# Half of the modulation sums of an experts' stage, split between GpSimd and ScalarE

## The reference, cut to what matters

```python
# first block: 4 groups of 8 experts, d = 1024, d_expert = 256, 256 tokens
hdn = jax.nn.silu(jnp.einsum('td,edf->tef', xc, w1)) * jnp.einsum('td,edf->tef', xc, w3)
ffn = jnp.einsum('tef,efd->td', hdn * gate[:, :, None], w2)
x = layernorm(DEEPNORM_ALPHA * x + g2 * ffn, ln2_g[l], ln2_b[l])

# second block: one row vector times a 1024 x 9216 matrix in each layer
c_act = jax.nn.silu(c)
mod = (c_act @ ada_w[i] + ada_b[i]).reshape(bsz, N_SUB, 3, d)
```

## Time and profile before

| | |
|---|---|
| median of 3 runs | 3307.97 us |
| lowest and highest | 3305.1 and 3314.28 us |
| profiled execution, its own time | 3315.41 us |
| its span in the trace | 3313.6 us |
| mean granted TensorE clock | 0.935 of full speed |
| the 40 steps of the stage, by the trace | about 225 to 620 us of the span |

### The profile page before, as it was taken

How to read it: one execution, slowest core, us unless ns; L and a number is a source line. 1 busy time by engine, 2 the same in 40 slices (tenths; PEclk the granted TensorE clock), 3 DMA queues, 4 the chain that set the end, 5 groups by cost and what they waited for, 6 DMA issues and landing times. The chain is left out here.

```text
span 3313.6 us, 58520 instructions
## 1 busy us (share of the span) xinstructions
PE 3078.3 (93%) x23850; PEld 2755.8 (83%) x23850; DVE 2410.0 (73%) x3506; ACT 1701.3 (51%) x2514; POOL 137.8 (4%) x164
## 2 busy tenths in 40 slices
PE   8879999799988899999988999999999999988899
PEld 7667777699877789899977898998689898878798
DVE  7769999788675478787665587885678787674655
ACT  5447777554552355545555445544654555432444
POOL 0110000000102000000010000000000001011000
PEclk9779999899999799999987999999899999998899
DMA  9629999668310378585420586773068586300542
GB/s 359 267 98 389 361 367 370 251 265 309 122 64 4 119 273 307 226 309 226 180 115 10 200 309 256 279 292 144 39 265 313 218 310 235 117 2 7 192 187 81
DMA packets 80297, 699.00 MB, mean 211 GB/s; under 512 B 8875, under 2 KB 12971, under 8 KB 58956
## 3 DMA queue, kind: packets, MB, share of 16 engines
q1 hardware_dynamic: 33708, 525.98, 40.6%
q10 hardware_dynamic: 42912, 157.31, 12.6%
q0 software_dynamic: 3456, 12.58, 1.0%
HBM read 691.64 MB, written 4.19 MB: 210 GB/s over the span
## 5 line engine op out<-in xcount | busy, mean ns | idle before, releaser
L1060 ACT ACTIVATE w_split<-ring 128x1024 fp32r<-128x1024 f32 x513 | 541.1, 1058 | 659.0 <-PE banks L984 391.2
L1167 DVE TENSOR_TENSOR w_split<-ring,w_split 128x1024 fp32r<-128x1024 f32 x513 | 625.6, 1223 | 274.7 <-ACT w_split L1060 266.7
L980 PE MATMUL banks<-u_split,w_split 128*128 128x512 f32 x2816 | 751.0, 399 | 23.7 <-DVE u_split L1236 21.0
L980 PEld LDWEIGHTS banks<-u_split,w_split 128*128 128x128 f32 x2816 | 517.4, 192 | 127.1 <-issue 17.6
L984 PE MATMUL banks<-u_split,w_split 128*128 128x256 f32 x2816 | 436.5, 285 | 0.0
L984 PEld LDWEIGHTS banks<-u_split,w_split 128*128 128x128 f32 x2816 | 406.9, 194 | 25.0
L973 PE MATMUL banks<-h_split,w_split 128*128 128x256 f32 x1408 | 398.5, 283 | 0.0
L974 PE MATMUL banks<-h_split,w_split 128*128 128x256 f32 x1408 | 398.5, 283 | 0.0
L975 PE MATMUL banks<-h_split,w_split 128*128 128x256 f32 x1408 | 398.4, 283 | 0.0
L526 PE MATMUL banks<-bufs_split,ring_split 128*128 128x256 f32 x1376 | 397.7, 289 | 0.0
L590 DVE CUSTOM_DVE_ANT_0 bufs<-bufs 128x1024 f32<-128x1024 f32 x288 | 341.9, 1220 | 12.0 <-DVE w_split L1167 12.0
(11 more groups left out here) (516 smaller groups left out, 4961.8 us busy)
## 6 DMA issues: line engine op xcount, KB each, us to landing
ring<-stream SPq DMA_DIRECT2D x153, 3072.0 KB, 10.9
bufs<-ada ACTq DMA_DIRECT2D x296, 512.0 KB, 10.3
bufs<-ada POOLq DMA_DIRECT2D x19, 512.0 KB, 7.5
bufs<-ada SPq DMA_DIRECT2D x16, 512.0 KB, 8.6
ring<-stream SPq DMA_DIRECT2D x8, 768.0 KB, 10.2
ring<-stream SPq DMA_DIRECT2D x2, 2688.0 KB, 9.9
bufs<-c_rows SPq DMA_DIRECT2D x10, 512.0 KB, 4.4
ring<-stream SPq DMA_DIRECT2D x1, 2704.0 KB, 10.0
```

Of the source, the lines that this page charges most:

```text
L980: pe.matmul(bank, w_split[:, slot, 0, k * P:(k + 1) * P], u_split[:, k, :, :], start=(k == 0), stop=False, skip_group_check=True)
L1060: nc.scalar.activation(w_split[:, slot, 0, :], piece(j, b), ACT.Copy).then_inc(high.sem, 1)
L1167: e = nc.vector.tensor_tensor(w_split[:, slot, 1, :], piece(j, b), w_split[:, slot, 0, :].bitcast(F32), ALU.subtract)
```

## The change

Quarters with an even number stay as they are on VectorE. A quarter with an odd number is done in two instructions on two engines: GpSimd multiplies it by the row `c` in place, as soon as it has landed (`tensor_tensor`, 128 x 1024, both inputs in SBUF), and ScalarE copies it over itself with an accumulated output (`activation` with `accum_out`). ScalarE does this at the end of step `q + 1`, ahead of that step's load. GpSimd's eight additions keep their order among the products: a product stands ahead of an addition of the same step. The load of a quarter now waits for the sum of the one four before it on the engine that makes it. The addition of the bias for `g2` moves from the end of step 8 to the end of step 9.

```diff
+    def quarter_sum(q):
+        at = 5 * KC + q if q < gate_quarters else q - gate_quarters
+        return core.mod_sums[:, at:at + 1]
...
+        multiplied, odd_step = core.event("k_products"), core.event("gate_sums")
...
             def load_quarters(step_of):
                 for q in ada_quarters(step_of):
                     if q >= 4:
-                        act.wait_ge(step.sem, step.at(q - 3))
+                        summed = odd_step if q % 2 else step
+                        act.wait_ge(summed.sem, summed.at(q // 2 - 1))
...
+            def sum_odd_quarter(q):
+                act.wait_ge(multiplied.sem, multiplied.at(q // 2 + 1))
+                slot = ada_slot[:, (q % 4) * D:(q % 4 + 1) * D]
+                act.activation(slot, slot, ACT.Copy, accum_out=quarter_sum(q)).then_inc(odd_step.sem, odd_step.count(1))
...
                 if e == 5 and v < WINDOWS - 1:
                     window_high(v + 1)
+                for q in ada_quarters(j):
+                    if q % 2:
+                        sum_odd_quarter(q)
                 if j >= first_quarter:
                     load_quarters(j + 3)
...
-            for i in range(2 * WINDOWS - 2):
+            def add_scaled(i):
                 pool.wait_ge(y_scaled.sem, y_scaled.at(i + 1))
                 rows = core.x[:, 4 * (i % 2):4 * (i % 2) + 4, :].rearrange("p c t -> p (c t)")
                 pool.tensor_tensor(rows, rows, scaled_y, ALU.add).then_inc(x_added.sem, x_added.count(1))
+
+            pool.wait_ge(c_ready.sem, c_ready.at(1))
+            for j in range(1, units + 1):
+                v, e = divmod(j, E)
+                for q in ada_quarters(j):
+                    if q % 2:
+                        pool.wait_ge(ada_loaded[q % 4].sem, ada_loaded[q % 4].at(16 * (q // 4 + 1)))
+                        slot = ada_slot[:, (q % 4) * D:(q % 4 + 1) * D]
+                        pool.tensor_tensor(slot, slot, gate_c_row if q < gate_quarters else c_row, ALU.mult)\
+                            .then_inc(multiplied.sem, multiplied.count(1))
+                if e in (2, 3) and 1 <= v < WINDOWS:
+                    add_scaled(2 * (v - 1) + e - 2)
...
             def sum_quarter(q):
-                dve.wait_ge(ada_loaded[q % 4].sem, ada_loaded[q % 4].at(16 * (q // 4 + 1)))
-                if q < gate_quarters:
-                    ada_quarter(core, dve, q % 4, ada_slot, gate_c_row, core.mod_sums[:, 5 * KC + q:5 * KC + q + 1])
-                else:
-                    at = q - gate_quarters
-                    ada_quarter(core, dve, q % 4, ada_slot, c_row, core.mod_sums[:, at:at + 1])
-                if q == gate_quarters - 1:
-                    dve.wait_ge(step.sem, step.at(gate_quarters))
+                if q % 2 == 0:
+                    dve.wait_ge(ada_loaded[q % 4].sem, ada_loaded[q % 4].at(16 * (q // 4 + 1)))
+                    ada_quarter(core, dve, q % 4, ada_slot, gate_c_row if q < gate_quarters else c_row, quarter_sum(q))
+                if q == gate_quarters:
+                    dve.wait_ge(step.sem, step.at(gate_quarters // 2))
+                    dve.wait_ge(odd_step.sem, odd_step.at(gate_quarters // 2))
                     dve.tensor_tensor(core.mod[:, 5 * KC:6 * KC], core.mod_sums[:, 5 * KC:6 * KC], core.col("b_ada")[:, 5 * KC:6 * KC], ALU.add)\
                         .then_inc(gate_ready.sem, gate_ready.count(1))
...
-            step.made += quarters
+            step.made += quarters // 2
```

## The result

| | before | after |
|---|---|---|
| median | 3309.45 us (4 runs) | 3343.9 us (4 runs) |
| lowest and highest | 3305.1 and 3314.28 us | 3338.38 and 3351.47 us |
| ratio to before | | 1.0106, 95% interval 1.0089 to 1.0123 |
| profiled execution, span | 3313.6 us | 3343.3 us |

A forecast was written before the change was run, and what follows sets the result against it. The prediction took VectorE to set the pace, with TensorE close behind. Between two sums, 22.6 and 35 us, it took 28 us of loss: 3308 + 28 = 3336 us, range 3315 to 3353 us.

The forecast's parts named there:

- The bound: In plain steps of 8.68 us, VectorE sets the pace and TensorE stands 0.17 to 0.3 us behind it.
- The price of a block: A GpSimd product meeting a fully working VectorE costs it 2.27 us, to save 1.14 us: 1.13 us net per moved quarter.
- Way (a): VectorE stays the bound throughout and all it saves is used: 20 x 1.13 = 22.6 us slower.
- Way (b): TensorE's lost waits: 7.5 us of blocks per window less 0.5 of relief, 7.0; 35 us over five windows.
- Where the products fall: Products start when loads land, at random places; one per window starts right behind the addition of step e = 3.
- ScalarE's copy: Copy plus accumulator read, 1.25 us twenty times, before the next step's first `high_part`; costed at nothing, 18 us at most.
- The signs to look for: `low_part` or sums of 1.3 to 3.5 us, products 2.4, TensorE's waits 40 or more, product-free plain steps near 8.5.
- the rival in which VectorE loses nothing: VectorE keeps the ports and GpSimd waits, products 3.5 us and more: no change, 3300 to 3308 us; chance 0.06.
- The relief does not win: Judges the rival that products fall into VectorE's idle time, 6.4 us per window: faster, 3300 us; chance 0.06.
- The blocks and the saving do not cancel: Judges the rival that VectorE's lead absorbs most of each block: 3308 to 3318 us; chance 0.11.
- The copy is not on the path: Judges the rival that ScalarE's copy adds up to 18 us to the forecast: 3354 us or more; chance 0.07.

The follow-up runs named there:

- Without products: The changed kernel with GpSimd's products left out, odd sums adding raw quarters, waits and copies kept; 3300.55 us, ratio 0.9972 to the kernel before.
- the placed product: Against the kernel before, only quarters 5, 13, 21 and 29 moved, each product waiting for step e = 5's last up piece; 3303.69 us, ratio 0.9988.
- short pieces: The changed kernel with each product split into four instructions of 256 columns; 3321.78 us, ratio 1.004 to the kernel before.
- half products: The changed kernel with products covering only the first 512 of 1024 columns; 3316.4 us, ratio 1.0021 to the kernel before.
- the products on top: The kernel before with all sums kept on VectorE and GpSimd's twenty products added; 3353.58 us, ratio 1.0132 to the kernel before.

## Why the prediction held, point by point

The prediction was 3336 us, 28 us over the median shown; measured were 34.5 us, inside its range of 3315 to 3353 us. It took the middle of two ways to add up. The measured total is that of the second way, 35 us, but in part by a term that neither had.

- **The bound.** Right. VectorE sets the pace in the plain steps with TensorE close behind. Without products the relief is worth 10 us by the medians, 5.4 us in the stage and 0.6 us per window (the prediction had 0.5 us per window), although 4 x 1.14 = 4.6 us of VectorE's work per window is gone.
- **The price of a block.** Right: 2.27 us predicted from one instruction of the trace; where a product holds one instruction of VectorE in full, it takes 3.40 us instead of 1.22, 2.18 us more. Not all meet one in full: in sum the twenty products make VectorE's instructions 39 us longer, 1.9 us each.
- **Way (a), 22.6 us.** It let all the saved work of VectorE count, and that was wrong: the relief brought 5 us in the stage, 10 by the medians, of 22.8 us, since TensorE is 0.2 to 0.3 us away in a plain step.
- **Way (b), 35 us.** Its terms for a window held: 7.5 us of blocks predicted, and 9.0 less 1.6 us of clock, 7.4 us, measured; 0.5 us of relief predicted, 0.6 measured. Step by step, against the kernel without products: 4.4 us in step e = 3, where two products fall (2.27 + 2.0 predicted), and 1.7 and 1.4 us for the other two (1.6 each predicted). What did not hold is the factor of five. By the windows the stage is longer by 3.4, 8.3, 8.5, 8.4 and 6.1 us, 34.7 in all: the first window has no additions and the last no gather.
- **The missing term.** TensorE's slower clock in step e = 4, 1.6 us in each of four windows, 6.4 us, was not in the prediction at all. Without it the stage's extra is 34.7 - 6.4 = 28.3 us. So the 28 us were about the price of the stalls, and the 6.5 us by which the forecast fell short have the size of this term. That the middle of two ways met the 28 us so well was largely luck: nothing made the truth lie between them, one way was wrong in its mechanism and the other counted a window too many.
- **Where the products fall.** Right for the one behind the addition of step e = 3. The next one was expected behind it, in a step with no lead, and lands still in the same step in each of the four windows, so that steps e = 2 and e = 3 are 4.4 us longer together. The places are not random either: from window to window each product starts within 1 us of the same place.
- **ScalarE's copy.** 1.05 + 0.19 us against 1.25 us predicted, and hidden, as costed.
- **The signs to look for.** VectorE's busy time went up and TensorE's waits for `low_part` to 45.1 us, as said. Two signs were read wrongly beforehand. A product is shown at 2.4 to 3.5 us and not at 2.4, as the time it waits for VectorE is within its span; 3.5 us had been called a sign of the rival in which VectorE loses nothing. And plain steps without a product take 9.2 to 9.3 us instead of "near 8.5": even without products the steps alternate between 7.7 and 9.25 us, because `product` of the relieved step comes earlier. Only a pair of steps can be compared with a pair.
- **The rivals.** The relief does not win: that needs the products in idle time, and the placed product shows it for one quarter in eight; the idle pieces of steps e = 2 and e = 3 were not tried. VectorE does not keep the ports through a row of instructions: the product gets its turn after one (the timeline of step e = 3). The blocks and the saving do not cancel, 40 us against 5 in the stage. The copy is not on the path, as the kernel without it shows.

## What to carry to other kernels

Before work is moved from VectorE to GpSimd, count the inputs that lie in SBUF: where GpSimd reads there and VectorE has both inputs there, GpSimd's instruction is added to VectorE's time, here up to 2.2 us to save 1.14. Such an operation belongs where VectorE waits or has an operand in PSUM, and it can be tied to that place by a semaphore of VectorE's own work; where that can't be had, short pieces cost half here. A look at the GpSimd operations that a kernel already has, with this in mind, was worth more here than the change.

## What the runs showed of the hardware that was not expected

**TensorE's clock.** TensorE's timeline of the changed kernel in step e = 3, on both sides of three holes:

```profile
434.74 0.39 PE L2087 MATMUL banks<-ring_split,bufs_split 128*128 128x512 f32 x1
436.60 0.47 PE L2085 MATMUL banks<-bufs_split 128*128 128x512 f32 x1 [1.47 <-DVE ring_split L2364]
...
437.82 0.39 PE L2087 MATMUL banks<-ring_split,bufs_split 128*128 128x512 f32 x1
439.83 0.50 PE L2085 MATMUL banks<-bufs_split 128*128 128x512 f32 x1 [1.62 <-DVE ring_split L2364]
...
441.12 0.39 PE L2087 MATMUL banks<-ring_split,bufs_split 128*128 128x512 f32 x1
444.39 0.47 PE L2085 MATMUL banks<-bufs_split 128*128 128x512 f32 x1 [2.89 <-DVE ring_split L2364]
```

And the busy time of stretches right after it, with the granted clock as the third number from the end:

```profile
444.00:446.00 2.00, 1.61 (x5) 1.34 (x6) 2.00 (x4) 0.00 (x0) 0.00 (x0) 0.76 0.88 369
446.00:448.00 2.00, 2.00 (x7) 1.51 (x6) 2.00 (x3) 0.82 (x2) 0.00 (x0) 0.50 0.97 418
448.00:450.00 2.00, 2.00 (x9) 1.60 (x9) 1.60 (x3) 1.27 (x2) 0.00 (x0) 0.88 1.03 442
450.00:452.00 2.00, 2.00 (x10) 1.66 (x9) 1.23 (x1) 2.00 (x4) 0.00 (x0) 1.00 0.81 270
```

After these holes, with 1.86, 2.01 and 3.27 us from start to start, the clock is at its lower level (1.2 of 2.4 GHz) for some 3 us, and TensorE starts 7 matmuls in 2 us where it starts 9 or 10 otherwise. In the stretches of the earlier trace rows the clock is full throughout. What it costs can be read from the kernel with half products, which meets both levels in the same step e = 4 of its four last windows:

```profile
345.08:352.78 7.70, 7.48 (x34) 6.21 (x35) 7.62 (x9) 5.56 (x9) 0.00 (x0) 1.00 0.88 375
427.52:435.24 7.72, 7.50 (x34) 6.22 (x35) 7.62 (x10) 5.56 (x9) 0.00 (x0) 1.00 0.89 374
510.15:519.44 9.29, 9.06 (x34) 7.35 (x35) 7.80 (x9) 5.55 (x9) 0.00 (x0) 0.82 0.86 358
594.37:602.09 7.72, 7.50 (x34) 6.22 (x35) 7.62 (x9) 5.57 (x9) 0.00 (x0) 1.00 0.86 369
```

One code and one place: 7.7 us at the full clock, 9.29 us where the mean clock is 0.82. The difference is 1.6 us. In the changed kernel all four windows have 0.82 and 9.28 to 9.30 us, without products all four 1.00 and 7.70 or 7.71. But the same holes don't always bring the lower level. With the products on top, step e = 3 has holes of 1.85, 2.0 and 3.3 us in all four windows, and step e = 4 behind it keeps the full clock in two of them:

```profile
357.66:366.34 8.68, 8.46 (x38) 7.04 (x39) 8.68 (x12) 5.86 (x7) 0.00 (x0) 1.00 0.89 377
445.84:454.52 8.68, 8.46 (x38) 7.03 (x39) 8.68 (x12) 5.86 (x7) 0.00 (x0) 1.00 0.85 362
534.09:544.76 10.67, 10.45 (x35) 8.37 (x36) 8.96 (x12) 5.07 (x7) 0.00 (x0) 0.70 0.73 293
625.11:634.69 9.58, 9.36 (x35) 7.62 (x36) 8.86 (x11) 5.23 (x7) 0.00 (x0) 0.82 0.83 342
```

What decides between the two isn't shown. A stall of an engine that feeds TensorE can cost more than its length, as here, and the surcharge is paid a step later, in a step in which nothing is blocked; whether it comes has to be looked up in the granted clock.

**The hand-over.** When GpSimd's instruction ends and both engines wait, VectorE goes first, and then GpSimd, in turns. It was so with products of 1024 columns (the timeline of step e = 3) and with pieces of 256.
